# The output product's second half in two rounds, and the first two experts' rows by one-hot products

## The reference, cut to what matters

```python
D_MODEL, SEQ, DEPTH, N_EXPERTS, TOP_K, D_EXPERT = 1024, 512, 2, 32, 2, 512
for l in range(DEPTH):
    # hybrid_mixer: three attention branches, gated and summed, then ONE output product
    y = (gates[:, :, 0] * (o_diff @ w_br[0]) + gates[:, :, 1] * (o_dsa @ w_br[1])
         + gates[:, :, 2] * (o_fox @ w_br[2]))
    m = y @ w_o                                            # 512 x 1024 x 1024
    h = layer_norm(DEEPNORM_ALPHA * h + m, ln1_g[l], ln1_b[l])
    # grouped_moe: router, best group of 4, two best experts in it
    aff = sigmoid(h @ w_router)
    sel = (aff + b_router).reshape(T, N_GROUPS, EXPERTS_PER_GROUP)
    g_idx = argmax(sum(top_k(sel, 2)))
    e_idx = two best experts of group g_idx ; wts = aff[e_idx] / sum
    # each expert: its rows of h
    hid = silu(rows @ w_gate[e]) * (rows @ w_up[e])
    f += wts * (hid @ w_down[e])
    h = layer_norm(DEEPNORM_ALPHA * h + f, ln2_g[l], ln2_b[l])
```

## Time and profile before

| what | value |
|---|---|
| median of three runs | 2340.98 us |
| profiled execution | 2343.16 us |
| its span | 2341.5 us |
| busy: PE, DVE, ACT, POOL | 88%, 40%, 28%, 8% |
| HBM read | 528.87 MB, 236 GB/s over the span |
| mean granted TensorE clock | 0.958 |

### The profile page before, as it was taken

One profiled execution on the slowest core, in us unless ns is written; L12 is line 12 of the kernel. 1 busy time (PEld: TensorE's weight loads), 2 busy tenths in 40 slices (PEclk: granted clock), 3 DMA queues, 4 the chain that ended last, 5 costly groups with the idle time before them and its releaser, 6 DMA issues.

```text
span 2341.5 us, 29179 instructions
## 1 busy us (share of the span) xinstructions
PE 2048.9 (88%) x9720; PEld 1185.9 (51%) x9728; DVE 935.6 (40%) x1817; ACT 656.8 (28%) x1361; POOL 194.6 (8%) x233
## 2 busy tenths in 40 slices
PE   4999999999989988788679999989999799887882
PEld 3776676577653332222257657757767333232220
DVE  5764745444561111111268566445446411110114
ACT  3444355354310100000143435445451111000000
POOL 0000001000011111111100000010000111111111
PEclk9999999999989999999879999999999899999996
DMA  5221221222479999999832113213234999999994
GB/s 174 88 89 37 72 74 71 72 72 73 198 293 407 425 425 426 425 426 425 349 114 84 62 37 108 72 37 108 73 114 174 380 425 424 425 425 426 426 425 197
DMA packets 96160, 536.18 MB, mean 229 GB/s; under 512 B 15984, under 2 KB 18800, under 8 KB 72448
## 3 DMA queue, kind: packets, MB, share of 16 engines
q1 hardware_dynamic: 83712, 511.06, 53.9%
q0 software_dynamic: 12288, 23.11, 2.6%
HBM read 528.87 MB, written 23.07 MB: 236 GB/s over the span
## 4 chain that ended last, share of the span: by engine, by line
PE 70%; DVE 9%; DMA 8%; issue 7%; ACT 2%; another core or an unknown queue 1%; POOL 1%; SPq 1%; DVEq 0%; ACTq 0%; POOLq 0%
PE ps L980 16%; PE ps L696 10%; PE ps L698 10%; PE ps L697 10%; PE ps L996 8%; PE ps L882 5%; DMA scr<-in_w_up 4%; PE ps L798 2%; DMA spare<-in_w_up 2%; PE ps L849 2%; PE ps L820 2%; PE ps L972 1%; DMA scr<-h_rows,scr 1%; DVE small L1530 1%
## 5 line engine op out<-in xcount | busy, mean ns | idle before, releaser
L1886 DVE COPY scr<-ps 128x512 f32<-128x512 f32 x66 | 45.6, 692 | 770.9 <-PE ps L972 770.9
L696 PE MATMUL ps<-hT_lo,w_hi 128*128 128x512 f32 (+1 forms) x832 | 339.1, 408 | 15.5 <-DVE w_lo L1392 7.4
L698 PE MATMUL ps<-hT_hi,w_hi 128*128 128x512 f32 (+1 forms) x832 | 327.5, 394 | 0.0
L697 PE MATMUL ps<-hT_hi,w_lo 128*128 128x512 f32 (+1 forms) x832 | 326.6, 393 | 0.0
L1110 ACT ACTIVATE scr<-ps 128x512 f32<-128x512 f32 (+3 forms) x296 | 129.8, 440 | 399.2 <-PE ps L996 305.9
L1130 ACT ACTIVATE w_hi<-ring 128x1024 fp32r<-128x1024 f32 x124 | 130.5, 1053 | 292.9 <-PE ps L698 231.0
L1392 DVE TENSOR_TENSOR w_lo<-ring,w_hi 128x1024 fp32r<-128x1024 f32 x124 | 150.7, 1216 | 132.5 <-ACT w_hi L1130 129.1
L696 PEld LDWEIGHTS ps<-hT_lo,w_hi 128*128 128x128 f32 (+1 forms) x832 | 157.1, 189 | 54.4 <-issue 8.3
L1332 ACT ACTIVATE scr<-ps 64x512 f32<-64x512 f32 x64 | 37.7, 589 | 523.7 <-PE ps L981 523.7
L698 PEld LDWEIGHTS ps<-hT_hi,w_hi 128*128 128x128 f32 (+1 forms) x832 | 156.9, 189 | 35.7
L882 PE MATMUL ps<-scr,ring 128*128 128x512 f32 x384 | 171.7, 609 | 3.4 <-ACT scr L1110 3.4
(11 more groups left out here) (245 smaller groups left out, 3212.3 us busy)
## 6 DMA issues: line engine op xcount, KB each, us to landing
ring<-in_w_down SPq DMA_DIRECT2D x32, 2048.0 KB, 48.3
ring<-in_w_in SPq DMA_DIRECT2D x30, 2048.0 KB, 7.6
xslot<-in_w_up SPq DMA_DIRECT2D x18, 2048.0 KB, 46.1
wslot<-in_w_gate SPq DMA_DIRECT2D x16, 2048.0 KB
ring<-in_w_gate SPq DMA_DIRECT2D x16, 2048.0 KB, 44.4
ring<-in_w_up SPq DMA_DIRECT2D x16, 2048.0 KB, 48.5
scr<-in_w_down SPq DMA_DIRECT2D x16, 2048.0 KB
scr<-in_w_up SPq DMA_DIRECT2D x14, 2048.0 KB
```

What stands on the lines that cost most here:

```text
L696: mm(out, a[0], b[1], start=first, stop=False)
L697: mm(out, a[1], b[0], start=False, stop=False)
L698: return mm(out, a[0], b[0], start=False, stop=last)
```

## The change

Four edits, cut to the core:

```diff
-CUT_FROM = 8
-        first_hot = scr[:, 13888:13888 + NT * C]
-        first_rank, first_empty = scr[:, 14144:14144 + NT], scr[:, 14148:14149]
-        first_idx = scr[:, 16516:16517].bitcast(U32)
+        first_hot = [scr[:, at:at + NT * C] for at in (13888, 16640)]
+        first_rank = scr[:, 14144:14144 + 2 * NT].rearrange("p (t e) -> p t e", e=2)
+        first_rows = [xin[0], score3[:, :]]
...
# SP, the first 12 pieces: one DMA each (no cuts), and
+                        elif s == MRING:
+                            sp.wait_ge(low_used.sem, low_used.at("m", l))
+                            alone(sp)
                         elif s == H_SLOT:
-                            multiplied("router")
+                            multiplied(("first", 1))
...
# PE, output(): the first half as before, then
+                    for t in range(NT):
+                        free(4 + t, l)
+                        for k in range(KD):
...
+                            ins = mm(bank[4 + t].t, y_lo[:, k, tok(t)], wo_hi(1, k), start=(k == 0), stop=False)
+                    ins.then_inc(low_used.sem, low_used.tick("m"))
+                    for t in range(NT):
+                        for k in range(KD):
+                            mm(bank[4 + t].t, y_hi[:, k, tok(t)], wo_lo(1, k), start=False, stop=False)
+                            ins = mm(bank[4 + t].t, y_hi[:, k, tok(t)], wo_hi(1, k), start=False, stop=(k == KD - 1))
+                        filled(ins, 4 + t, ("m", t, 1))
+                        if t >= 2:
+                            transpose_tile("ln1", t - 2, l)
...
# PE, route(): behind the router product of tile 3
+                    free(6, l)
+                    for _ in range(5):
+                        mm(bank[6].t, ident, cos, start=True, stop=True)
                     pe.wait_ge(hot_ready.sem, hot_ready.at("hot", l))
...
-                    pe.wait_ge(first_ready.sem, first_ready.at("hot", l))
-                    free(4, l)
-                    for t in range(NT):
-                        for half in range(2):
-                            ins = mm(bank[4].t[half * C:(half + 1) * C, 0:1], first_hot[:, t * C:(t + 1) * C],
-                                     place[:, 0, t:t + 1], start=(t == 0), stop=(t == NT - 1))
-                    filled(ins, 4, "first")
-
-                    free(6, l)
-                    for _ in range(6):
-                        mm(bank[6].t, ident, cos, start=True, stop=True)
-                    expert_rows(0, xin_land[0].start(l) + 16, l)
+                    for e in range(2):
+                        pe.wait_ge(first_ready.sem, first_ready.at(e, l))
+                        free(4 - e, l)
+                        for t in range(NT):
+                            for half in range(2):
+                                ins = mm(bank[4 - e].t[half * C:(half + 1) * C, :], first_hot[e][:, t * C:(t + 1) * C],
+                                         h[:, t, half * 512:(half + 1) * 512], start=(t == 0), stop=(t == NT - 1))
+                        filled(ins, 4 - e, ("first", e))
+                    for e in range(2):
+                        in_sbuf(4 - e, ("first", e), l)
+                        alone(pe)
+                        free(e, l)
+                        alone(pe)
+                        filled(turn_rows(first_rows[e], e), e, ("x", e))
...
# PE, expert_turn(): rows of expert 1 are there already, and "places" (L966) moves here
+                        if e:
+                            expert_rows(e + 1, xin_land[(e + 1) % 2].start(l, i) + 16 * ((e + 1) // 2), l, i)
                     gates(0)
+                    places(l, i)
...
# ACT, behind the sigmoid of tile 3
+                    for e in range(2):
+                        filled(4 - e, ("first", e), l)
+                        copy(first_rows[e], 4 - e, bank[4 - e].t)
+                    filled(0, ("x", 0), l)
+                    copy(xT[0], 0, bank[0].t.rearrange("p (k c) -> p k c", c=C))
...
# DVE: two one-hots instead of one; the index of expert 0 (L1730, L1731) goes; rows(1) instead of rows(0)
+                    for e in range(2):
+                        V.tensor_tensor(first_hot[e].rearrange("p (t b a) -> p t b a", t=NT, b=16),
+                                        spread.unsqueeze(1).to_broadcast([P, NT, 16, C // 16]),
+                                        first_rank[:, :, e].unsqueeze(2).unsqueeze(3).to_broadcast([P, NT, 16, C // 16]),
+                                        ALU.is_equal).then_inc(first_ready.sem, first_ready.tick(e))
...
# POOL: the gathers of experts 0 and 1 go
-                    gather_rows(0, xin_land[0], "x", first_idx)
                     pool.wait_ge(index_ready.sem, index_ready.at("x", l))
                     alone(pool)
-                    gather_rows(1, xin_land[1], "x", x_idx[:, 1:2])
```

More of the change, by code:

```diff
@@ L346, in trunk @@
         wo_ready = signal("wo_ready")
+        low_used = signal("low_used")
         aff_ready = signal("aff_ready")
@@ L591, in expert_piece @@
                         src = (w_gate, w_up, w_down)[m][one, e].rearrange("o q p c -> p (o q c)")
-                        for q in range(cuts):
-                            part = slice(q * PIECE // cuts, (q + 1) * PIECE // cuts)
-                            sp.dma_start(slots[s][:, part], src[:, part]).then_inc(land[s].sem, land[s].tick(key, 16))
+                        sp.dma_start(slots[s], src).then_inc(land[s].sem, land[s].tick(key, 16))
                     def used(n, i=NTURN - 1):
@@ L621, in _ @@
                             multiplied(("m", NT - 1, 1))
-                        expert_piece(n, ("first", n), 4 if n >= CUT_FROM else 1)
+                        expert_piece(n, ("first", n))
                     book.scope = "tail"
@@ L889, in product @@
                                              (wo_hi(half, k), wo_lo(half, k)), k == 0, k == KD - 1)
-                    for half in range(2):
-                        for t in range(NT):
[L893 to L905, removed]
+                    for t in range(NT):
+                        free(4 + t, l)
+                        for k in range(KD):
+                            if t == 0:
+                                pe.wait_ge(wo_ready.sem, wo_ready.at((0, k), l))
+                                alone(pe)
+                                pe.wait_ge(y_ready.sem, y_ready.at(("y", k), l))
+                                alone(pe)
+                            ins = product(t, 0, k)
+                        filled(ins, 4 + t, ("m", t, 0))
@@ new lines, in output @@
+                    for t in range(NT):
+                        free(4 + t, l)
+                        for k in range(KD):
+                            if t == 0:
+                                pe.wait_ge(wo_ready.sem, wo_ready.at((1, k), l))
+                                alone(pe)
+                            ins = mm(bank[4 + t].t, y_lo[:, k, tok(t)], wo_hi(1, k), start=(k == 0), stop=False)
+                    ins.then_inc(low_used.sem, low_used.tick("m"))
+                    for t in range(NT):
+                        for k in range(KD):
+                            mm(bank[4 + t].t, y_hi[:, k, tok(t)], wo_lo(1, k), start=False, stop=False)
[3 more added lines that the diff above has]
+                            transpose_tile("ln1", t - 2, l)
@@ L946, in route, with places @@
                     filled(ins, 5, "rank")
-                    pe.wait_ge(first_ready.sem, first_ready.at("hot", l))
-                    free(4, l)
-                    for t in range(NT):
-                        for half in range(2):
-                            ins = mm(bank[4].t[half * C:(half + 1) * C, 0:1], first_hot[:, t * C:(t + 1) * C],
-                                     place[:, 0, t:t + 1], start=(t == 0), stop=(t == NT - 1))
-                    filled(ins, 4, "first")
-                    free(6, l)
-                    for _ in range(6):
-                        mm(bank[6].t, ident, cos, start=True, stop=True)
-                    expert_rows(0, xin_land[0].start(l) + 16, l)
+                    for e in range(2):
+                        pe.wait_ge(first_ready.sem, first_ready.at(e, l))
+                        free(4 - e, l)
+                        for t in range(NT):
+                            for half in range(2):
[4 more added lines that the diff above has]
+                        in_sbuf(4 - e, ("first", e), l)
+                        alone(pe)
+                        free(e, l)
+                        alone(pe)
+                        filled(turn_rows(first_rows[e], e), e, ("x", e))
+                def places(l, i):
                     pe.wait_ge(dve_seq.sem, dve_seq.at("places", l))
-                    free(5, l)
+                    free(5, l, i)
                     for k in range(2):
@@ L968, in route, with turn_rows @@
                     filled(ins, 5, "places")
-                def turn_rows(n, b):
+                def turn_rows(rows, b):
```

(12 more changed lines are left out.)

10 lines of the change are left out of this document (3 added, 7 removed).

## The result

The changed kernel takes 2351.93 us (median of 5, 2350.78 to 2353.73) against 2340.72 for the kernel before on the same chip: 1.0047 times, 95% interval 1.0036 to 1.0058, +11.2 us. In a second comparison beside the experiments (`after_again`, expected at +8 to +12 us) the same kernel gave 1.0028 (1.0017 to 1.0040), +6.6 us; one of its twelve executions took 3913.6 us at a granted clock of 0.818 and is left out as slow. The intervals only just overlap, so the change costs somewhere between 0.2 and 0.6%; which of the two is nearer, no run decides. Slower, as forecast; the profiled execution took 2351.06, span 2349.3.

What follows compares the result with a forecast made beforehand. Bound: the expert weight stream, solid from piece 13's issue. Rank's start +6.9 us, less row-product and second-hole gains, plus 0.4 a layer of gather traffic, gave +3.0 and +5.1, together +8.1: 2349 us, range 2339 to 2356.

Steps and rivals of the forecast that it cites:

- What bounds the kernel: Expert weight stream: a layer's end moves with T, piece 13's issue, plus the second hole; earlier transfers don't count.
- signs of being wrong: Wrong if rank's start moves under 3 us, the stream isn't solid after piece 13's issue, or its end doesn't follow that.
- Part 1: Two rounds in the second half: VectorE's norms become the bound, tile 2's transposes end later, +2.9 us for all that follows.
- The clock: TensorE's new wait before the router product: half clock there and in part of the neighbouring work, +2.0 us, between 0 and +3.4.
- Fillers: Five filler matmuls ahead of rank hold back its start R: +2.0 us, between 0 and +4.7.
- Part 3: Expert rows by products: piece 13 goes out 17.4 us after rank's start R, 2.6 and 1.8 us less than before.
- Second hole: Stream after piece 13: pieces 15 and 16 go out 8.2 us later, so the hole closes, -1.7 and -0.4 us.
- 0, or 1 us if the gather is slow: Expert 2's later gather: TensorE waits 1 to 4 us, but 19.6 us of queued pieces cover it.
- Sum: Both layers: +3.0 in layer 1 and +5.1 in layer 2, together +8.1 us, 2349 us on the median's scale.
- (1): Rival: clock holds through the router product, or fillers are hidden; 2341 to 2345 us, chance 0.24.
- (2): Rival: VectorE's later tiles are hidden, rank's start stays, layers gain 3.9 and 1.8 us; 2335 us, chance 0.12.
- (3): Rival: clock falls again between rank and the products, +1.7 to +3.4 us a layer more; 2352 to 2356 us, chance 0.12.

Runs made afterwards that it cites:

- delay_T: Kernel before with four more filler matmuls right ahead of expert 0's gate and up product; 1.0030 times the kernel before, +7.0 us.
- late_slot: Changed kernel, but slot 3's first piece waits for the last tile as before, the two rounds kept; 1.0040 times the kernel before.
- tile0_first: Changed kernel with tile 0's 24 second-half matmuls first and whole, then low and high rounds of tiles 1 to 3; 1.0004 times the kernel before.
- no_fill: Changed kernel without the five filler matmuls ahead of rank; 1.0030 times the kernel before.
- products_fill4: Changed kernel with the old tile-after-tile second half, slot 3 released by the last tile, and four fillers instead of five; 0.9990 times the kernel before.

## Why the prediction was right, step by step

- **What bounds the kernel**: right. T moves a layer's end (delay_T), traffic before T does not (late_slot, and the standing DMA engines at 693). "From there on the stream is solid" held for the kernel before only: in the changed one a small hole came 28 us after T, one of the prediction's own signs of being wrong.
- **Part 1, +2.9 us from the norms**: right. The norms run back to back, 5.0 us each (5.13 assumed), the last starts 3.3 us later than before. Tile 2's transposes end at M + 27.5; at full clock before it was M + 24.6, which is the 2.9. tile0_first takes back the 1.4 us that its order should.
- **The clock, +2.0**: right in place, high in size. L926 took 2.79 us, as long as in late_slot, where the clock was at 0.50 throughout: half clock costs it 1.3 us, not the 1.5 of a doubling. The clock was back before L935, and tile 2's transposes lost nothing. Together with the norms top-k is 4.0 us late, not 4.9. In late_slot it is 5.1 and 5.5 in the two layers, in no_fill 5.5: the prediction's figure was in the range, but which of these patterns came was not its doing. Whether transposes count as the engine being busy, on which the prediction quotes the Trainium skill (TensorE: Matmul & The Clock Gate, Part 4: PE-mode transpose), these runs don't decide: the wait itself was idle too.
- **Fillers, +2.0**: 1.6. R moved by 5.6 us, not 6.9, inside the bounds 2.9 to 11.
- **Part 3, T = R + 17.4**: measured 17.5 and 17.4; both products 7.09 us for 6.9 + the last one's end.
- **Second hole, -1.7 and -0.4, and "0, or 1 us if the gather is slow"**: this is the step that failed. The old hole went, but TensorE waited 3.3 us for expert 2's rows (1 to 4 were forecast), its clock fell to 0.50 and the down product took 5.67 us, so piece 17 went out 19.1 us after T, not 15 to 18, at the edge of the 19.6 us that were queued, and piece 18 after it (26 us after T, with 24.5 queued) opened a new hole. The clock's fall behind that wait was put at nothing; products_fill4, where the clock was back sooner, piece 17 went out 1.1 us earlier and no hole came, shows that this was the term. Over both layers the stream gained nothing where 1.3 us net were expected.
- **Sum**: +4.0 and +4.3 us at the last down product, together 8.3, where 3.0 + 5.1 = 8.1 was forecast. That they agree so closely is luck. T moved by 3.1 + 3.8 = 6.9 us, 2.5 less than the forecast's 9.4 because R moved by less, and the 1.3 us of the holes did not come back; the remaining 1.4 us between T and the last down product are within that column's scatter. The median moved by 11.2 us in one comparison and by 6.6 in the other, the profiled pair by 7.9; no run shows what makes these differ. Of the rivals, (1), the clock holds, is out for this kernel, but tile0_first shows that an order with the norms 1.4 us earlier is enough for it; (2), the norms hidden, is out; (3), a second fall between rank and products, did not come in any kernel: in no_fill part of the products ran at half clock because it had been at 0.50 since M + 26.3.

## What to carry to other kernels

When a stream of loads through a fixed number of slots bounds a stage, find the one use from which it runs without a hole: time before that use is free for transfers, and most of the latency in front of it is paid (3.6 and 4.1 us later gave +7.0 us in delay_T). A product regrouped into rounds that run over all tiles keeps its length but completes its first tiles later; if another engine was just keeping up tile by tile, all of its work now stands at the end. A wait of 2 to 3 us on TensorE can cost more than itself, because what follows may run at half clock, so count both, also behind waits that look hidden: a queue that covers the wait may not cover the slow product behind it.

## What the runs showed of the hardware that was not expected

Fillers put into a wait are two-sided: ahead of rank they cost 1.5 us of latency and saved 2.0 us of products at half clock. The point at which the clock falls in one and the same order of work moved by 1.7 us between kernels and layers (M + 26.3 to M + 28.0), worth 1.4 to 2.9 us at top-k, while in any one execution top-k starts alike in both layers to 0.4 us.

How long the clock then stays down is as little settled by the order of work. In the changed kernel it fell at M + 27.8, L926 took 2.79 us, and at 673 the clock was at 1.00 again. In late_slot L921, the same product, took the same 2.79 us with nearly the same pauses on both sides (0.69 and 0.94 us for 0.74 and 0.94), and the clock stayed at 0.50 for 12 us more. The product by itself, then, is not what brings the clock back; what does, these runs leave open. The changed kernel's window in which L926 ends (at 672.6), and the next:
```profile
672.00:673.00 1.00, 0.63 (x4) 0.00 (x0) 1.00 (x2) 0.30 (x1) 0.00 (x0) 0.61 1.06 446
673.00:674.00 1.00, 0.43 (x4) 0.46 (x5) 0.00 (x0) 0.19 (x1) 0.47 (x1) 1.00 0.98 414
```
